# Two more load places for the first expert's chunks, and its first split set ahead of the last exponentials, in a one-core encoder block with 16 experts

## The chip, the cores and the metric

The kernel runs on one core of one Trainium2 chip. The metric is the device time of an execution in microseconds (us), the median of several runs. Engines are named PE (TensorE; PEld is its weight load), DVE (VectorE), ACT (ScalarE), POOL (GpSimd) and SP (SyncE). SP issues most DMAs, POOL the indirect ones.

## The reference

Two sets of 512 tokens of 1024 features in float32 go through one encoder layer: two groups of attention heads, their output projection added to the input, then a mixture of 16 experts in which every expert chooses its tokens.

```
def expert_choice_moe(h, w_router, w_gate, w_up, w_down):
    xf = h.reshape(n, d)                       # n = 512, d = 1024
    aff = jax.nn.softmax(jnp.einsum('nd,de->ne', xf, w_router), axis=-1)
    gates, idx = lax.top_k(aff.T, cap)         # cap = 2 * n / 16 = 64
    xe = xf[idx]
    hid = jax.nn.silu(jnp.einsum('ecd,edf->ecf', xe, w_gate)) * jnp.einsum('ecd,edf->ecf', xe, w_up)
    ye = jnp.einsum('ecf,efd->ecd', hid, w_down) * gates[..., None]
    y = jnp.zeros_like(xf).at[idx.reshape(-1)].add(ye.reshape(-1, d))

def encoder_layer(x, p):
    ...                                        # attention
    x = x + jnp.einsum('bse,ed->bsd', o, p['w_o'])
    h2 = rms_norm(x, p['norm_ffn'])
    return x + expert_choice_moe(h2, p['w_router'], p['w_gate'], p['w_up'], p['w_down'])
```

`w_gate`, `w_up` and `w_down` are 16 x 1024 x 1024 each, 201 MB together.

## The kernel before

There are four stages on one core: the input projection, attention, routing (`route`) and the experts (`experts`). No scheduler orders the work: each engine's program is written out by hand, the stages follow each other in it, and engines meet by semaphores.

**Two-part products.** Every large product is made of three in a faster format (`fp32r`): a tile is split into a higher part `hi` (ACT, a copy that rounds) and a lower part `lo` (raw minus `hi`), and hi x hi, lo x hi and hi x lo are added in PSUM.

**Chunks.** The experts' weights come in chunks of 128 x 2048 (1 MB, two blocks of 128 rows): 8 of gate and up per expert (`GU_CHUNKS`), in turns, then 4 of down. `load_chunk` issues one; those of expert 0's gate and up go as four DMAs of 32 partitions each, because its rows are stored in another order. Before the change there are `RING` = 6 places `raw` for loads, and 6 each of `hi` and `lo`. `split` of ACT (L2204) makes `hi`, `split` of DVE (L2282) makes `lo`, POOL the very first one (L2065). PE uses a chunk for 12 products of 512 columns (`gate_up`, `down`) and then counts `chunk_used`, which frees its place of `hi` and `lo`. `at(e, j)` numbers all chunks: 0 to 7 are expert 0's gate and up, from 8 on come expert 1's eight and the four of down of expert 0, and so on. ACT and DVE work `AHEAD` = 5 chunks ahead of PE. SP's `load` waits until `lo_done` has counted the chunk that had the place, six before.

**Routing.** Eight tiles of 128 tokens go through in the order 0, 1, 4, 5, 2, 6, 3, 7. For each, PE makes the output projection, DVE adds the residual (`x1`), SP stores it to `out`, ACT and POOL make the normalised rows `h2` (ACT `scale_rows`, L1766; POOL times the gain, L1605), SP stores them, and PE, ACT and DVE make the logits and the softmax (`exponentials`, L1760). SP issues chunks 0 to 5 among the tiles (`sync_program`, `load_chunk` of chunk j - 2 with tile j). After the last tile DVE finds the 64 largest per expert, and PE turns the lists. POOL then gathers expert 0's rows into `xe` (L2070), PE transposes them (L2184, L2091), ACT and DVE split them (into `hthi`, `htlo`), and PE's first expert product starts. While the lists are made, PE runs 24 transposes without use (L2180).

**Experts.** In the turn of expert e, PE makes gate and up (L2114 to L2116), eight transposes of the hidden rows of expert e - 1 (L2091) and down of e - 1 (L2128 to L2130). The next expert's rows are gathered by four DMAs (L2050), turned by DVE (`xt`, L2298) and split into `xehi` (ACT, L2212) and `xelo` (DVE, L2293). DVE makes `xelo` behind the lower part of the next expert's third chunk. POOL adds the rows of results to `out` by an indirect DMA (L2060).

**Memory.** `raw` lies in `arena`, where projected rows lay before; `hi` and `lo` over the buffers of attention and routing. `hi2` covers `h2` buffers, so ACT's third split waits for the last `h2` store.

Of the kernel before, what the change touches and what calls it, by code (L numbers as in the profile page):

```python
# [20 lines left out]
P = 128  # L21
# [30 lines left out]
RING = 6  # L52
# [69 lines left out]
def build(nc, a, out):  # L122
# [11 lines left out]
    with ExitStack() as ctx:  # L134
# [9 lines left out]
        k["ones"] = sb("ones", [P, 1])  # L144
        k["tab"] = sb("tab", [P, TS, TAB])
# [3 lines left out]
        k["gkp"] = sb("gkp", [P, TS, 2, PE_D])  # L149
        k["gcol"] = sb("gcol", [P, G_ROWS])  # L150
# [141 lines left out]
        moe["raw"] = [mm(f"raw{i}", [P, CHUNK]) for i in range(RING)]  # L292
        assert mm.at <= temps_at
# [1173 lines left out]
def route(phase, a, x_dram, k, wo, moe, ps, banks, o_dram, r_dram, out_rows, h2_rows, raw_loaded, attend_signals):  # L1467
# [40 lines left out]
    lmax_done, nbias_done, lexp_done, lrec_done, aff_done = sem("lmax_done"), sem("nbias_done"), sem("lexp_done"), sem("lrec_done"), sem("aff_done")  # L1508
    at_ready, at_done, merged, psteps, vsteps = sem("at_ready"), sem("at_done"), sem("merged"), sem("pool_steps_r"), sem("vector_steps_r")
# [32 lines left out]
    def sync_program(sp):  # L1542
# [13 lines left out]
        for u in range(T - 3, T):  # L1556
            store_rows(sp, u)
            store_scaled(sp, u)

    def gpsimd_pieces(pool):  # L1560
# [20 lines left out]
        def rest():  # L1581
# [7 lines left out]
            for j in range(1, T + 1):  # L1589
# [127 lines left out]
    def scalar_pieces(act):  # L1717
# [51 lines left out]
        def rest():  # L1769
# [16 lines left out]
            square_half(1)  # L1786
            exponentials(LAST)
# [178 lines left out]
    route_signals = {"merged": merged, "x1_stored": x1_stored, "h2_stored": h2_stored, "h2_done": h2_done}  # L1966
# [3 lines left out]
def experts(phase, a, k, moe, ps, banks, out, h2_dram, raw_loaded, route_signals):  # L1970
# [12 lines left out]
    merged, x1_stored, h2_stored, h2_done, rows_set = (  # L1983
        route_signals[n] for n in ("merged", "x1_stored", "h2_stored", "h2_done", "rows_set"))
# [13 lines left out]

    def loads_of(e, j):
        parts = P // SQUARE  # L2000
        if isinstance(e, int) and e == 0:
            return parts * (j // RING + 1)
        first = 2 if slot_of(e, j) < GU_CHUNKS - RING else 1
        return CHUNKS // RING * e + (j - DOWN_CHUNKS) // RING + 1 + (parts - 1) * first

    sem = phase.sem
    hi_done, lo_done, chunk_used = sem("hi_done"), sem("lo_done"), sem("chunk_used")
# [10 lines left out]
    def sync_program(sp):  # L2018
        need_split = sp.alloc_register("need_split")

        def load(e, j, name, of, i):
# [4 lines left out]
            load_chunk(sp, a, moe, raw_loaded, slot_of(e, j), name, of, i)  # L2026
# [12 lines left out]
    def gpsimd_program(pool):  # L2039
# [24 lines left out]
        pool.wait_ge(hi_done, 1)  # L2064
        pool.tensor_tensor(lo[0][:], raw[0][:], hi[0][:].bitcast(F32), ALU.subtract).then_inc(lo_done, 1)  # L2065
# [132 lines left out]
    def scalar_program(act):  # L2198
        def split(e, j):
            s = slot_of(e, j)  # L2200
            act.wait_ge(raw_loaded[s], 16 * loads_of(e, j))
            if not (isinstance(e, int) and e == 0 and j < RING):
                act.wait_ge(chunk_used, at(e, j) - RING + 1)
            act.activation(hi[s][:], raw[s][:], ACT.Copy).then_inc(hi_done, 1)  # L2204
# [38 lines left out]
        for j in range(RING):  # L2243
# [195 lines left out]
```

## Time and profile before

| | us |
|---|---|
| median of 3 runs | 1070.81 (1070.47 to 1073.97) |
| profiled execution | 1069.35 |
| its span, first to last instruction | 1067.5 |
| PE busy | 1022.0 (96%) |
| DVE busy | 888.9 (83%) |
| ACT busy | 771.1 (72%) |
| POOL busy | 494.8 (46%) |

The trace gives for every instruction its start in us from the span's start, its duration, and for idle time before it the operation that released it. Tile names stand without their numbers: `lo<-raw,hi` is any chunk's lower part, `h<-h,gffn` the rows `h2` times their gain. A DMA's time runs from the issue on SP or POOL to its landing. PEclk is the granted TensorE clock as a share of 2.4 GHz, the DMA share the mean busy share of the 16 DMA engines. Matmuls are shown longer than their distance, since they overlap. The attention stage ends near 350 us, routing runs to about 500, the experts to the end.

### The profile page before, as it was taken

How to read it: one execution, taken by the hardware profiler on the slowest of the kernel's cores; microseconds unless marked ns; L12 is line 12 of the kernel's file. 1: busy time of each engine (PE TensorE's matmuls, PEld its weight loads, DVE VectorE, ACT ScalarE, POOL GpSimd, SP SyncE). 2: the span in 40 equal slices, each digit the busy share in tenths (PEclk: the TensorE clock that was granted, in tenths of full speed). 3: DMA queues.
4: the chain of work that ended last, by engine and by line, in shares of the span. 5: the costliest groups of instructions: out<-in, count | busy, mean ns of one | idle time of the engine just before them, and what ended most of it. 6: DMA issues, size and time to landing. Idle time of an engine off the chain costs nothing.

```text
span 1067.5 us, 16503 instructions
## 1 busy us (share of the span) xinstructions
PE 1022.0 (96%) x5401; PEld 866.5 (81%) x5401; DVE 888.9 (83%) x1123; ACT 771.1 (72%) x1071; POOL 494.8 (46%) x458
## 2 busy tenths in 40 slices
PE   8999998999999999995999999999999999999995
PEld 7999987888788888884778888888787777877784
DVE  6787669999999954478999999889998999889992
ACT  7655568999999834335777887777877787778771
POOL 2476479555699754344442343224432343224021
PEclk9999999999999999996999999999999999999998
DMA  8132050211331379724999999999999999999992
GB/s 310 68 127 106 1 200 11 51 33 39 110 112 59 113 190 281 222 95 124 365 405 390 388 407 390 393 389 389 407 392 390 388 408 390 392 389 399 400 365 40
DMA packets 90128, 270.30 MB, mean 253 GB/s; under 512 B 16273, under 2 KB 24684, under 8 KB 89820
## 3 DMA queue, kind: packets, MB, share of 16 engines
q1 hardware_dynamic: 84272, 252.34, 62.9%
q0 software_dynamic: 5744, 17.29, 6.6%
q8 instruction: 28, 0.46, 0.2%
q14 instruction: 24, 0.20, 0.1%
q10 hardware_dynamic: 60, 0.01, 0.0%
HBM read 243.27 MB, written 26.35 MB: 253 GB/s over the span
## 4 chain that ended last, share of the span: by engine, by line
DVE 16%; DMA 15%; PE 12%; issue 8%; ACT 3%; POOLq 0%; DVEq 0%; POOL 0%; SPq 0%
DMA raw<-in_w_down 14%; DVE lo L2282 12%; PE ps L2114 3%; PE ps L2116 3%; PE ps L2115 3%; ACT hi L2204 2%; DVE h L2304 1%; DVE xelo L2293 1%; PE ps L2130 1%; PE ps L2128 1%; PE ps L2129 1%; DVE xt L2298 1%; DMA out<-y,give 1%; DMA xe<-h,idxT 0%; PE ps L2091 0%
## 5 line engine op out<-in xcount | busy, mean ns | idle before, releaser
L2282 DVE TENSOR_TENSOR lo<-raw,hi 128x2048 fp32r<-128x2048 f32 x191 | 431.9, 2287 | 40.5 <-ACT hi L2204 40.4
L2204 ACT ACTIVATE hi<-raw 128x2048 fp32r<-128x2048 f32 x192 | 367.6, 1919 | 109.3 <-DMA raw<-in_w_down 59.2
L2114 PE MATMUL ps<-hi,xehi 128*128 128x512 f32 x480 | 189.3, 394 | 7.6 <-DVE xelo L2293 6.6
L2116 PE MATMUL ps<-hi,xelo 128*128 128x512 f32 x480 | 187.1, 390 | 0.0
L2115 PE MATMUL ps<-lo,xehi 128*128 128x512 f32 x480 | 186.9, 389 | 0.0
L2045 POOL COPY take<-idx 128x4 uint32 (+1 forms) x15 | 29.0, 1935 | 208.1 <-DVE xt L2298 203.4
L2050 POOL DMA_INDIRECT xe<-h,take x60 | 104.9, 1748 | 25.1 <-issue 13.7
L2114 PEld LDWEIGHTS ps<-hi,xehi 128*128 128x128 f32 x480 | 90.1, 188 | 30.1 <-DVE lo L2282 9.1
L2116 PEld LDWEIGHTS ps<-hi,xelo 128*128 128x128 f32 x480 | 90.1, 188 | 18.9
L2115 PEld LDWEIGHTS ps<-lo,xehi 128*128 128x128 f32 x480 | 90.2, 188 | 18.0
L1417 DVE TENSOR_TENSOR probTlo<-ps,probThi 128x512 fp32r<-128x512 f32 x128 | 87.6, 684 | 14.1 <-ACT probThi L1372 11.5
L1363 ACT ACTIVATE prob<-ps,nmax 128x512 f32<-128x512 f32 x128 | 88.8, 693 | 7.8 <-DVE nmax L1421 6.7
L2128 PE MATMUL ps<-hi,hthi 128*128 128x512 f32 x240 | 93.5, 389 | 0.0
L2130 PE MATMUL ps<-hi,htlo 128*128 128x512 f32 x240 | 93.4, 389 | 0.0
L2129 PE MATMUL ps<-lo,hthi 128*128 128x512 f32 x240 | 93.4, 389 | 0.0
L1421 DVE TENSOR_REDUCE nmax<-ps 128x1 f32<-128x512 f32 x128 | 87.3, 683 | 4.2 <-PE ps L1255 2.5
L1268 PEld LDWEIGHTS ps<-ident,prob 128*128 128x128 f32 x512 | 62.6, 141 | 25.6 <-issue 7.9
L2060 POOL DMA_INDIRECT out<-y,give x15 | 32.2, 2145 | 110.1 <-ACT y L2240 110.1
L1372 ACT ACTIVATE probThi<-ps 128x512 fp32r<-128x512 f32 x128 | 76.8, 600 | 8.5 <-PE ps L1268 7.6
L1268 PE MATMUL ps<-ident,prob 128*128 128x128 f32 x512 | 77.1, 273 | 4.8 <-DVE probTlo L1417 4.4
L503 POOL TENSOR_TENSOR small<-small,minus_half 128x1 f32<-128x1 f32 (+4 forms) x40 | 66.1, 1653 | 3.3
L1286 PE MATMUL ps<-probThi,v 128*128 128x256 f32 x256 | 56.3, 301 | 0.0
(302 smaller groups left out, 2167.5 us busy)
## 6 DMA issues: line engine op xcount, KB each, us to landing
raw<-in_w_down SPq DMA_DIRECT2D x64, 1024.0 KB, 13.2
raw<-in_w_gate SPq DMA_DIRECT2D x60, 1024.0 KB, 11.2
raw<-in_w_up SPq DMA_DIRECT2D x60, 1024.0 KB, 11.5
w_raw<-in_w_in SPq DMA_DIRECT2D x8, 592.0 KB, 8.9
x<-in_x SPq DMA_DIRECT2D x8, 512.0 KB, 3.9
r<-reciprocal_sums SPq DMA_DIRECT2D x32, 128.0 KB, 2.9
attention_out<-pj SPq DMA_DIRECT2D x16, 256.0 KB, 2.5
woraw<-in_w_o SPq DMA_DIRECT2D x4, 1024.0 KB, 5.6
```

The lines of the kernel that those rows point to most:

```text
L1268: turned = pe.transpose(ps[:, T_BANKS[u % 2], cols], att["p"][u % 3][:, cols], k["ident"][:])
L1363: act.activation(att["p"][v % 3][:], ps[:, S_BANKS[v % 3], :], ACT.Exp, bias=att["nmax"][:, v:v + 1], accum_out=att["sum"][:, v:v + 1]).th ...
L1417: dve.tensor_tensor(ptlo[v // 2 % 2][:, :, cols], ps[:, T_BANKS[v % 2], :].rearrange("p (a c) -> p a c", a=TS), pthi[v // 2 % 2][:, :, col ...
L2050: pool.indirect_dma_start(xe[:, q * PART:(q + 1) * PART], None, h2_quarters, bass.IndirectOffsetOnAxis(moe["take"][:, q:q + 1], 0)).then_i ...
L2114: pe.matmul(ps[:, dst[n], :], rowhi[:, c, :], hi[w][:, cols], start=c == 0, stop=False)
L2115: pe.matmul(ps[:, dst[n], :], rowhi[:, c, :], lo[w][:, cols], start=False, stop=False)
L2116: last = pe.matmul(ps[:, dst[n], :], rowlo[:, c, :], hi[w][:, cols], start=False, stop=c == KD - 1)
L2128: pe.matmul(ps[:, Y[n], :], hthi[:, f, :], hi[w][:, cols], start=f == 0, stop=False)
L2129: pe.matmul(ps[:, Y[n], :], hthi[:, f, :], lo[w][:, cols], start=False, stop=False)
L2130: last = pe.matmul(ps[:, Y[n], :], htlo[:, f, :], hi[w][:, cols], start=False, stop=f == KD - 1)
L2204: act.activation(hi[s][:], raw[s][:], ACT.Copy).then_inc(hi_done, 1)
L2282: dve.tensor_tensor(lo[s][:], raw[s][:], hi[s][:].bitcast(F32), ALU.subtract).then_inc(lo_done, 1)
```

## The change

- Two more places for loads: `raw6` over the rotary tables and gains, which only the projection reads, and `raw7` over the start of the lower part of the output weights. `h` and `y` of the experts move over `raw7`, which is read for the last time before they are written.
- Chunks 6 and 7 go into these places and are issued in routing: chunk 6 ahead of the store of tile number 5, chunk 7 ahead of the store of tile number 6, when `wo_done` has counted the first group of products of the last tile. Each place has one load of expert 0 only; later chunks use six places again (`raw_of`).
- Expert 1's chunks 8 to 13 now follow into places 0 to 5, each when the lower part of chunk 0 to 5 is made. From chunk 14 on the rule is as before: the lower part of the chunk six earlier. The twelve loads of expert 1's turn are written out, the loop starts with expert 2.
- ACT makes `hi` of chunk 0 ahead of the last tile's exponentials and rows. POOL makes `lo` of chunk 0 ahead of the last tile's rows times gain, and `lo` of chunk 1, which DVE made before, behind them.

The diff, cut to its core:

```
@@ sync_program of route
         for u in range(T - 3, T):
+            c = RING + u - (T - 3)
+            if c < GU_CHUNKS:
+                if c > RING:
+                    sp.wait_ge(wo_done, 2 * LAST + 1)
+                load_chunk(sp, a, moe, raw_loaded, c, GATE_UP[c % 2], 0, c // 2)
             store_rows(sp, u)
             store_scaled(sp, u)
@@ gpsimd_pieces, rest
+                if u == LAST:
+                    pool.wait_ge(hi_done, 1)
+                    pool.tensor_tensor(moe["lo"][0][:], moe["raw"][0][:], moe["hi"][0][:].bitcast(F32), ALU.subtract).then_inc(lo_done, 1)
                 pool.wait_ge(h2_scaled, u + 1)
@@ scalar_pieces, rest
             square_half(1)
+            act.wait_ge(raw_loaded[0], 16 * (P // SQUARE))
+            act.activation(moe["hi"][0][:], moe["raw"][0][:], ACT.Copy).then_inc(hi_done, 1)
             exponentials(LAST)
@@ experts
+    def raw_of(e, j):
+        return j if isinstance(e, int) and e == 0 else j % RING
@@ sync_program of experts
-        for j in range(RING, GU_CHUNKS):
-            load(0, j, GATE_UP[j % 2], 0, j // 2)
-        with sp.Fori(1, EXPERTS) as e:
+        for j in range(CHUNKS):
+            sp.wait_ge(lo_done, j + 1 if j < RING else at(1, j) - RING + 1)
+            name, of, i = (GATE_UP[j % 2], 1, j // 2) if j < GU_CHUNKS else ("w_down", 0, j - GU_CHUNKS)
+            load_chunk(sp, a, moe, raw_loaded, raw_of(1, j), name, of, i)
+        with sp.Fori(2, EXPERTS) as e:
@@ gpsimd_program
-        pool.wait_ge(hi_done, 1)
-        pool.tensor_tensor(lo[0][:], raw[0][:], hi[0][:].bitcast(F32), ALU.subtract).then_inc(lo_done, 1)
+        pool.wait_ge(hi_done, 2)
+        pool.tensor_tensor(lo[1][:], raw[1][:], hi[1][:].bitcast(F32), ALU.subtract).then_inc(lo_done, 1)
@@ scalar_program
-        for j in range(RING):
+        for j in range(1, RING):
@@ vector_program
-        dve.wait_ge(lo_done, 1)
-        for j in range(1, RING):
+        dve.wait_ge(lo_done, 2)
+        for j in range(2, RING):
```

ACT at the end of routing, before; `x1_1` is the last tile, `aff1` its softmax, `hi0` the higher part of chunk 0:

```order
L1747 ACTIVATE sqo_123,smallo_115<-x1_1_127 128x512 [waits x1_done_p]
L1760 ACTIVATE aff1_118,smallo_115<-ps,smallo_115 128x16 [waits at_ready_p,aff_cleared_p,nbias_done_p]
L1766 ACTIVATE h2_1_134<-x1_1_127,smallo_115 128x8x4x32 [waits h2_stored1_p,r2_done_p]
L2204 ACTIVATE hi0_145<-raw0_139 128x2048 [waits raw_loaded0]
L2204 ACTIVATE hi1_146<-raw1_140 128x2048 [waits raw_loaded1]
L2204 ACTIVATE hi2_147<-raw2_141 128x2048 [waits raw_loaded2,h2_stored1_p,h2_stored0_p]
```

And now, with the line numbers of the changed kernel:

```order
L1762 ACTIVATE sqo_123,smallo_115<-x1_1_127 128x512 [waits x1_done_p]
L1803 ACTIVATE hi0_147<-raw0_139 128x2048 [waits raw_loaded0]
L1775 ACTIVATE aff1_118,smallo_115<-ps,smallo_115 128x16 [waits at_ready_p,aff_cleared_p,nbias_done_p]
L1781 ACTIVATE h2_1_134<-x1_1_127,smallo_115 128x8x4x32 [waits h2_stored1_p,r2_done_p]
L2225 ACTIVATE hi1_148<-raw1_140 128x2048 [waits raw_loaded1]
L2225 ACTIVATE hi2_149<-raw2_141 128x2048 [waits raw_loaded2,h2_stored1_p,h2_stored0_p]
```

The split of chunk 0 has moved ahead of the exponentials and the rows.

POOL at the same place, before (`pow` for the last norm, rows times gain, lower part 0, gather of expert 0's rows):

```order
L1566 TENSOR_TENSOR smallo_115<-smallo_115,minus_half 128x1 [waits pool_steps_r_p]
L1605 TENSOR_TENSOR h2_1_134<-h2_1_134,gffn_135 128x1024 [waits aff_done_p,h2_scaled_p]
L2065 TENSOR_TENSOR lo0_151<-raw0_139,hi0_145 128x2048 [waits hi_done_p]
L2070 DMA xe_157<-h2,idxT_166 128x1024 [waits h2_stored1_p,x1_stored1_p,idx_ready_p,h2_stored0_p,x1_stored0_p]
```

And now:

```order
L1578 TENSOR_TENSOR smallo_115<-smallo_115,minus_half 128x1 [waits pool_steps_r_p]
L1616 TENSOR_TENSOR lo0_153<-raw0_139,hi0_147 128x2048 [waits hi_done_p]
L1620 TENSOR_TENSOR h2_1_134<-h2_1_134,gffn_135 128x1024 [waits aff_done_p,h2_scaled_p]
L2086 TENSOR_TENSOR lo1_154<-raw1_140,hi1_148 128x2048 [waits hi_done_p]
L2091 DMA xe_159<-h2,idxT_162 128x1024 [waits h2_stored1_p,x1_stored1_p,idx_ready_p,h2_stored0_p,x1_stored0_p]
```

Lower part 0 stands ahead of the rows, and a lower part 1 between the rows and the gather.

SP from the load of chunk 5 on, before:

```order
L1527 DMA h2<-h2_0_133 128x1024 [waits h2_done_p]
L1523 DMA out<-x1_1_127 128x1024 [waits x1_done_p]
L1527 DMA h2<-h2_1_134 128x1024 [waits h2_done_p]
L1523 DMA out<-x1_0_126 128x1024 [waits x1_done_p]
L1527 DMA h2<-h2_0_133 128x1024 [waits h2_done_p]
L1523 DMA out<-x1_1_127 128x1024 [waits x1_done_p]
L1527 DMA h2<-h2_1_134 128x1024 [waits h2_done_p]
L1461 DMA raw0_139<-in_w_gate 32x2x1024 [waits lo_done_p,raw_loaded0]
L1461 DMA raw0_139<-in_w_gate 32x2x1024 x3
L1461 DMA raw1_140<-in_w_up 32x2x1024 [waits lo_done_p,raw_loaded0]
L1461 DMA raw1_140<-in_w_up 32x2x1024 x3
```

And now:

```order
L1534 DMA h2<-h2_0_133 128x1024 [waits h2_done_p]
L1467 DMA raw6_145<-in_w_gate 32x2x1024 x4
L1530 DMA out<-x1_1_127 128x1024 [waits x1_done_p]
L1534 DMA h2<-h2_1_134 128x1024 [waits h2_done_p]
L1467 DMA raw7_146<-in_w_up 32x2x1024 [waits wo_done_p]
L1467 DMA raw7_146<-in_w_up 32x2x1024 x3
L1530 DMA out<-x1_0_126 128x1024 [waits x1_done_p]
L1534 DMA h2<-h2_0_133 128x1024 [waits h2_done_p]
L1530 DMA out<-x1_1_127 128x1024 [waits x1_done_p]
L1534 DMA h2<-h2_1_134 128x1024 [waits h2_done_p]
L1470 DMA raw0_139<-in_w_gate 128x2x1024 [waits lo_done_p]
L1470 DMA raw1_140<-in_w_up 128x2x1024 [waits lo_done_p]
```

Chunks 6 and 7 have moved ahead of the stores of `x1`, and expert 1's chunks follow the last `h2` store, without chunks of expert 0 between.

## Rows read from the trace of the kernel before

**Rows 1.** Busy PE, PEld, DVE, ACT, POOL (count); clock, DMA share, GB/s
```profile
458.00:470.00 12.00, 12.00 (x66) 10.03 (x65) 7.03 (x20) 5.72 (x10) 5.51 (x6) 1.00 0.23 89
502.00:506.00 4.00, 4.00 (x21) 4.00 (x20) 3.94 (x9) 1.79 (x1) 1.12 (x1) 0.50 0.89 228
541.00:734.00 193.00, 192.86 (x871) 159.78 (x870) 178.77 (x108) 151.93 (x113) 72.67 (x41) 1.00 1.03 395
734.00:1010.00 276.00, 270.69 (x1216) 222.25 (x1216) 252.79 (x152) 214.33 (x160) 88.18 (x51) 1.00 1.03 394
```

**Rows 2.** Waits of TensorE's products, 720 to 1020: us, times, longest
```profile
PE ps L2114 <- DVE xelo L2293: 6.1, 9, 0.8
```

**Rows 3.** Waits of ScalarE, 540 to 610, then 650 to 1010
```profile
ACT hi L2204 <- PE ps L2116: 7.2, 11, 0.9
...
ACT hi L2204 <- DMA raw<-in_w_down: 48.4, 42, 2.5
```

**Rows 4.** Timeline of TensorE: start, us; the eight transposes of three experts
```profile
638.53 1.04 PE L2091 MATMUL ps<-ident,h 128*128 128x128 f32 x8
...
672.07 1.04 PE L2091 MATMUL ps<-ident,h 128*128 128x128 f32 x8
...
1016.23 1.04 PE L2091 MATMUL ps<-ident,h 128*128 128x128 f32 x8
```

**Rows 5.** Timeline of SyncE's queue: stores of the last tiles, chunks 6 to 8
```profile
458.31 0.43 SPq L1523 DMA_DIRECT2D out<-x  x1
...
493.81 0.32 SPq L1527 DMA_DIRECT2D h<-h  x1
498.36 1.93 SPq L1461 DMA_DIRECT2D raw<-in_w_gate  x4
505.26 1.90 SPq L1461 DMA_DIRECT2D raw<-in_w_up  x4
507.64 0.42 SPq L1464 DMA_DIRECT2D raw<-in_w_gate  x1
```

**Rows 6.** Timeline of ScalarE at the end of routing; in brackets idle time
```profile
489.86 0.36 ACT L1760 ACTIVATE aff<-ps,smallo 128x16 f32<-128x16 f32 x1 [2.25 <-DVE smallo L1855]
...
496.48 7.31 ACT L2204 ACTIVATE hi<-raw 128x2048 fp32r<-128x2048 f32 x4 [1.53 <-issue]
507.39 0.38 ACT L2252 ACTIVATE hthi<-ps 128x256 fp32r<-128x256 f32 x1 [3.59 <-PE ps L2184]
```

**Rows 7.** Timeline of GpSimd at the end of routing
```profile
491.43 2.35 POOL L1605 TENSOR_TENSOR h<-h,gffn 128x1024 f32<-128x1024 f32 x1 [2.62 <-ACT h L1766]
493.75 4.52 POOL L2065 TENSOR_TENSOR lo<-raw,hi 128x2048 fp32r<-128x2048 f32 x1
502.28 1.12 POOL L2070 DMA_INDIRECT xe<-h,idxT  x1 [4.01 <-DVE idxT L2329]
```

**Rows 8.** Timeline of VectorE: expert 0's token numbers; its run of lower parts
```profile
501.03 0.37 DVE L2329 TENSOR_SCALAR idxT<-ps 64x16 uint32<-64x16 f32 x2
...
509.28 17.70 DVE L2282 TENSOR_TENSOR lo<-raw,hi 128x2048 fp32r<-128x2048 f32 x8
```

**Rows 9.** Issue to landing of `raw` loads: 540 to 570, 507 to 512
```profile
DMA to landing us min/median/max: 8.8/9.4/11.3
...
DMA to landing us min/median/max: 6.9/8.0/8.7
```

**Rows 10.** Issue to landing: `woraw`'s four loads; gathers into `xe`, 500 to 530
```profile
DMA to landing us min/median/max: 5.1/5.6/7.1
...
DMA to landing us min/median/max: 4.6/7.2/8.0
```

**Rows 11.** Timeline of TensorE: warm-up, turning of expert 0's rows, first product
```profile
501.34 5.38 PE L2180 MATMUL ps<-ident 128*128 128x128 f32 x24
506.91 0.66 PE L2184 MATMUL ps<-ident,xe 128*128 128x128 f32 x4 [0.19 <-DMA xe<-h,idxT]
...
508.49 0.47 PE L2114 MATMUL ps<-hi,hthi 128*128 128x512 f32 x1 [0.48 <-DVE htlo L2351]
```

More of the change, by code:

```diff
@@ L144, in build @@
         k["ones"] = sb("ones", [P, 1])
+        tables_at = (nc.sbuf_base + 63) // 64 * 64
         k["tab"] = sb("tab", [P, TS, TAB])
@@ L149, in build @@
         k["gkp"] = sb("gkp", [P, TS, 2, PE_D])
+        assert nc.sbuf_base >= tables_at + CHUNK * 4
         k["gcol"] = sb("gcol", [P, G_ROWS])
@@ L292, in build @@
         moe["raw"] = [mm(f"raw{i}", [P, CHUNK]) for i in range(RING)]
+        moe["raw"] += [Map(tables_at)("raw6", [P, CHUNK]), Map(w_in_end)("raw7", [P, CHUNK])]
         assert mm.at <= temps_at
@@ L311, in build @@
         moe["give2"] = mm("give2", [P, 2], U32)
+        assert mm.at <= w_in_end
+        mm.at = w_in_end
+        moe["h"] = mm("h", [P, FF])
+        moe["y"] = mm("y", [P, D])
+        assert mm.at == w_in_end + CHUNK * 4
+        moe["xelo"] = mm("xelo", [P, KD, P], F32R)
+        moe["silu"] = mm("silu", [P, FF])
+        moe["hthi"] = mm("hthi", [P, KD, P], F32R)
+        moe["htlo"] = mm("htlo", [P, KD, P], F32R)
+        moe["xt"] = mm("xt", [P, D])
         assert mm.at <= end, (mm.at, end)
-        raw_loaded = [ctx.enter_context(nc.semaphore(f"raw_loaded{i}")) for i in range(RING)]
+        raw_loaded = [ctx.enter_context(nc.semaphore(f"raw_loaded{i}")) for i in range(GU_CHUNKS)]
         wo_loaded = ctx.enter_context(nc.semaphore("wo_loaded"))
@@ L1982, in experts @@
     TAIL = GU_CHUNKS + CHUNKS * LAST
-    merged, x1_stored, h2_stored, h2_done, rows_set = (
-        route_signals[n] for n in ("merged", "x1_stored", "h2_stored", "h2_done", "rows_set"))
+    hi_done, lo_done, merged, x1_stored, h2_stored, h2_done, rows_set = (
+        route_signals[n] for n in ("hi_done", "lo_done", "merged", "x1_stored", "h2_stored", "h2_done", "rows_set"))
     out_halves = out.rearrange("t (h c) -> (t h) c", h=2)
@@ L2001, in loads_of @@
         if isinstance(e, int) and e == 0:
-            return parts * (j // RING + 1)
-        first = 2 if slot_of(e, j) < GU_CHUNKS - RING else 1
-        return CHUNKS // RING * e + (j - DOWN_CHUNKS) // RING + 1 + (parts - 1) * first
+            return parts
+        return CHUNKS // RING * (e - 1) + j // RING + 1 + parts
     sem = phase.sem
-    hi_done, lo_done, chunk_used = sem("hi_done"), sem("lo_done"), sem("chunk_used")
+    chunk_used = sem("chunk_used")
     route_ready, gates_ready, idx_ready = sem("route_ready"), sem("gates_ready"), sem("idx_ready")
@@ L2199, in split @@
         def split(e, j):
-            s = slot_of(e, j)
-            act.wait_ge(raw_loaded[s], 16 * loads_of(e, j))
+            s, r = slot_of(e, j), raw_of(e, j)
+            act.wait_ge(raw_loaded[r], 16 * loads_of(e, j))
             if not (isinstance(e, int) and e == 0 and j < RING):
                 act.wait_ge(chunk_used, at(e, j) - RING + 1)
-            act.activation(hi[s][:], raw[s][:], ACT.Copy).then_inc(hi_done, 1)
+            act.activation(hi[s][:], raw[r][:], ACT.Copy).then_inc(hi_done, 1)
         def high(dst, b, ready, n, done):
```

16 lines of the change are left out of this document (5 added, 11 removed).

## The prediction

> **What bounds the kernel now.** I read the stretches first [rows 1]. From 541 to 1010 us, nearly half of the span, the DMA engines are full (share 1.03, 394 to 395 GB/s). TensorE is also at 192.86 of 193 us until 734, but at 270.69 of 276 us after that. So two limits lie close together: TensorE sets the pace first, the weight transfers later.
>
> The waits say the same. From 720 us on, TensorE's first product of an expert waits nine times for VectorE's `xelo` [rows 2]. VectorE writes `xelo` after the lower part of the next expert's third chunk, and that one waits for ScalarE's higher part. Up to 610 us ScalarE's splits wait for TensorE to free `hi`; from 650 us on they wait for landings [rows 3]. An expert's eight transposes are a good marker of pace [rows 4]: 672.07 - 638.53 = 33.54 us where TensorE sets it. From 672.07 to 1016.23 are ten experts: 344.16 us, against 335.4 at that pace. **So 8.8 us is all that an earlier stream of weights can win back**, and only if TensorE starts no later. After 1016 the end is TensorE's own work and does not move against it.
>
> **The change part by part.** I number expert 0's gate and up chunks 0 to 7 and go on with expert 1's from 8.
>
> 1. *Chunks 6 and 7 are issued in the routing stage.* Now they go out at 498.36, when GpSimd has made the first lower part, and at 505.26, after VectorE's first [rows 5]. Four parts each take 1.9 us to issue. In the changed kernel chunk 6 goes ahead of the store at 458.31, where the DMA engines are busy 0.23 of the time [rows 1], and chunk 7 after the last tile's first group of products. The stores behind them on SyncE's queue are needed only by the gather at 502.28, twenty us later; that cover costs nothing. What leaves is two chunks of the crowded stretch after 498.
>
> 2. *Higher part 0 ahead of the last exponentials.* ScalarE is idle for 2.25 us from 487.6 to 489.86, and one split takes 1.9 us (7.31 us for four, less overlap) [rows 6]. It ends about 489.5 and the exponentials start as before: 0.
>
> 3. *Lower part 0 on GpSimd ahead of the last `h2` rows.* GpSimd then works 489.6 to 494.1 (4.52 us), makes the rows until 496.45 (2.35 us, now 491.43 to 493.78), then lower part 1 until 501.0 [rows 7]. Two things hang on it. The store of `h2`, issued at 493.81 now [rows 5], goes at 496.5, 2.7 us later. ScalarE's third split, which starts 2.7 us after that issue (496.48), moves to 499.2, and four splits end at 506.5; the next work waits until 507.39 [rows 6], so 0.9 us of cover is left: 0. If the store lands over 0.9 us later than that, every us more delays TensorE. The gather of expert 0's rows is queued behind lower part 1. It waits for its indices, which VectorE has written at 501.4 [rows 8], and starts at 502.28: 0.4 us of cover, cost 0; any lengthening beyond this goes into TensorE's start one to one.
>
> 4. *VectorE loses lower part 1.* It is no gain: VectorE still makes part 2 at 502.9, then waits for the gathered rows, and its run of eight lower parts starts at 509.28 as now [rows 8]. The two waits of TensorE near 531 and 535 us hang on that run; they stay.
>
> 5. *Expert 1's loads go out earlier.* Chunk 8 waits for lower part 0 alone, but stands behind the `h2` store: 496.8. Chunk 9 goes when lower part 1 is done, 501.1, chunk 10 at 505.2, against 507.64 for chunk 8 now [rows 5]. Chunks 11 to 13 need VectorE's run, 17.70 us for eight, and go at 511.6, 513.8 and 516.0. Chunk 14 needs lower part 8 in both kernels: same time. By then the queue should be empty, which it isn't now.
>
> **How far ahead can the stream get?** This is the step that I chose on. It would be two chunks plus their slow four-part form, over 5 us. But chunks from 14 on are issued when a place is free, that is at TensorE's pace, in both kernels, and nothing lands sooner than a lone chunk takes. Of the chunks issued from 540 to 570 the quickest lands after 8.8 us [rows 9]. Lone loads of the same 1024 KB, of `woraw`, take 5.1 to 5.6 us [rows 10]; I take 5.6, its upper value, since gathers run beside the weights too. So the lead is 8.8 - 5.6 = **3.2 us**, bounds 8.8 - 5.1 = 3.7 and, where a gather comes first as well, 8.8 - 6.2 = 2.6. From there the queue is never empty again, so the lead lasts until it is spent on the nine waits, of 8.8 us together: it removes the first three to four.
>
> The Trainium skill (DMA: Bandwidth & Descriptors, "Anatomy of one DMA — SWDGE (gpsimd) path") gives a DMA a fixed part of about 2.0 us and bytes over 436 GB/s, an estimate of 4.4 us for such a chunk. The rows show 5.1 at best; by the rule the lead would be 4.4 us, and the time 1067.3.
>
> **What chunk 9 costs the gather.** The gather of expert 0's rows takes 4.6 us (502.28 to 506.9) on nearly empty queues, and TensorE starts 0.19 us after it [rows 10, 11]. In the changed kernel chunk 9 was issued 1.2 us before it. At 395 GB/s a chunk keeps the queues for 2.7 us, from some 502.5 to 505.2, and the gather's 512 KB, 1.3 us at that rate, would flow from about 504 on. That is 0 to 1.2 us of delay for TensorE's first product (508.49). I take **0.9 us**, nearer to the upper end, because the later gathers, of 128 KB each on full queues, take 7.2 us in the median although they are a quarter of the size.
>
> The skill's same page ("Queues, rings and completion order") says that an engine drains a whole packet of some 9 to 17 descriptors from one queue before it turns to the next. By that rule chunk 9's share passes whole and the delay is the full 1.2 us; that no row here shows.
>
> **Sum.** -3.2 + 0.9 = -2.3 us, with 0 for splits, stores and VectorE. The profiled execution took 1069.35 us (span 1067.5), so it would be about 1067.0. The median of the runs is 1070.81, 1.5 us above the profiled one; the same difference gives **1068.5 us**. Bounds: -3.7 + 0 and -2.6 + 1.2, that is 1067.1 to 1069.4.
>
> **The rivals.** *A larger lead.* The `h2` store of 512 KB has landed 2.7 us after its issue (493.81 to ScalarE's 496.48); another 512 KB at the full rate make 4.0 us. If a lone chunk lands in 4.5, between this and 5.1, the lead is 4.3, and without a delay of the gather the time is 1066.5. Against it: none of the four loads of `woraw` came under 5.1. The skill's fixed part, above, points to this case; by it and with no delay the time would be 1066.4.
>
> *No lead.* The chunks issued in 507 to 512 took 6.9 to 8.7 us with one or two ahead of them [rows 9]. If about 8 us is what a chunk takes in this stage whatever is queued, the lead is 8.8 - 8 = 0.8 and the gather takes it back: 1070.9. The same time comes if VectorE, and not the landings, holds `xelo` back: then an earlier stream changes nothing. Against that: ScalarE's waits for landings in [rows 3].
>
> *Slower, by a late gather and a slow clock.* A quarter gather would take 4.6 - 1.0 = 3.6 us alone and takes 7.2 on a full queue. If the first gather is held up as much by chunk 9, TensorE starts 3.6 us later, which alone eats the 3.2. TensorE would also stand idle that long after its warm-up transposes, which run from 501.34 for 5.38 us [rows 11], at a granted clock of 0.50 [rows 1] (1.2 GHz). If the clock falls again in that gap, the first products pay as the transposes did: about 5.4 us at half speed are 2.7 us lost. Time 1070.8 + 0.4 + 2.7 = 1073.9. It decides from the gap at which the clock falls; the gaps of 0.19 and 0.48 us there now let it stand, and 0.9 more should.
>
> **How the numbers follow.** The sum above 0.55, own range 1067.1 to 1069.4; the larger lead 0.20 at 1066.5; no lead 0.14 at 1070.9; the slower one 0.11 at 1073.9. Predicted is 1068.5. The range of 8 in 10 takes in the first three but for their tails: 1066.0 to 1071.5. A measurement of this kernel can tell about 0.3%, 3.2 us: faster is under 1067.6, slower over 1074.0. Faster gets one in six of the first case (0.09) and nearly all of the second (0.19): 0.28. Slower gets half of the last, rounded up: 0.06. Within it 0.66.
>
> **What would show it.** Right: chunks 6 and 7 issued from 458 on and before 486; exponentials still at 489.9; gather issued at 502.3, landing 507 to 508; TensorE's first product at 508.5 to 509.7; the quickest chunk from 540 to 570 landing after 5.2 to 6 us; experts at 33.54 us until well past 800; five to six waits for `xelo` in place of nine, and 8.8 us of loss down to about 5.6. The forecast is wrong if TensorE's first product is over 2 us late (part 3, or the gather), if the minimum landing stays above 8 us, or if TensorE waits for something new, such as the two reused places, after 541.

## The result

| | before | after |
|---|---|---|
| median, us | 1070.95 (20 runs) | 1073.89 (20 runs) |
| profiled span, us | 1067.5 | 1072.1 |
| first expert product of TensorE | 508.49 | 513.77 |
| TensorE's waits for `xelo`, 720 to 1020 us | 9 | 8 |

The changed kernel is slower: ratio 1.0026, 95% interval 1.0015 to 1.0036, or 2.9 us. Forecast was 1068.5 with a range of 1066.0 to 1071.5, so the time lies outside it and on the other side of before. The ratios here and below leave out three slow executions, of 1287 us (fourth experiment), 2648 us (fifth) and 3643 us (sixth).

Where does it go? VectorE's timeline at the end of routing, after (start in us, duration, then the instruction; `smallo` holds the routing's small columns). L1869 takes the largest logit, L1872 multiplies it by the root, which gives the bias of the exponentials:

```profile
490.60 0.17 DVE L1869 TENSOR_REDUCE smallo<-ps 128x1 f32<-128x16 f32 x1 [1.16 <-PE ps L1695]
490.81 4.33 DVE L1872 TENSOR_TENSOR smallo<-smallo 128x1 f32<-128x1 f32 x1
```

The same product before the change:

```profile
489.67 0.16 DVE L1855 TENSOR_TENSOR smallo<-smallo 128x1 f32<-128x1 f32 x1
```

L1872 works on 128 x 1 elements and takes **4.33 us**, where it took 0.16. In the changed kernel it also takes 0.16 us for the tile before. GpSimd's timeline at the same time:

```profile
490.63 4.49 POOL L1616 TENSOR_TENSOR lo<-raw,hi 128x2048 fp32r<-128x2048 f32 x1 [0.69 <-ACT hi L1803]
496.75 2.35 POOL L1620 TENSOR_TENSOR h<-h,gffn 128x1024 f32<-128x1024 f32 x1 [1.62 <-ACT h L1781]
499.06 4.50 POOL L2086 TENSOR_TENSOR lo<-raw,hi 128x2048 fp32r<-128x2048 f32 x1
507.59 1.12 POOL L2091 DMA_INDIRECT xe<-h,idxT  x1 [4.03 <-DVE idxT L2350]
```

GpSimd's lower part 0 (L1616) starts at 490.63 and ends at 495.12. VectorE's product starts 0.18 us later and ends 0.02 us after it. ScalarE then shows who waits:

```profile
488.66 1.89 ACT L1803 ACTIVATE hi<-raw 128x2048 fp32r<-128x2048 f32 x1
495.18 0.36 ACT L1775 ACTIVATE aff<-ps,smallo 128x16 f32<-128x16 f32 x1 [4.62 <-DVE smallo L1872]
...
502.14 7.31 ACT L2225 ACTIVATE hi<-raw 128x2048 fp32r<-128x2048 f32 x4 [3.67 <-issue]
```

The exponentials start at 495.18 after 4.62 us of idle time, where [rows 6] had 489.86. Everything behind them is 5.3 to 5.7 us later than before: the `h2` rows at 496.75 (491.43 in [rows 7]), the gather at 507.59 (502.28), the last four splits at 502.14 (496.48). TensorE's timeline (warm-up transposes, turning of expert 0's rows, first products):

```profile
506.65 4.21 PE L2201 MATMUL ps<-ident 128*128 128x128 f32 x24
512.20 0.66 PE L2205 MATMUL ps<-ident,xe 128*128 128x128 f32 x4 [1.34 <-DMA xe<-h,idxT]
...
513.77 0.47 PE L2135 MATMUL ps<-hi,hthi 128*128 128x512 f32 x1 [0.48 <-DVE htlo L2372]
514.08 0.40 PE L2136 MATMUL ps<-lo,hthi 128*128 128x512 f32 x1
514.31 0.40 PE L2137 MATMUL ps<-hi,htlo 128*128 128x512 f32 x1
```

The first product comes at 513.77, 5.28 us later than in [rows 11]. Of these, 1.14 are there before the change has done anything, as SyncE's queue shows (store of `h2` rows, chunk 6, last `h2` store, chunks 8 and 9):

```profile
459.04 0.34 SPq L1534 DMA_DIRECT2D h<-h  x1
459.43 2.23 SPq L1467 DMA_DIRECT2D raw<-in_w_gate  x4
...
499.12 0.32 SPq L1534 DMA_DIRECT2D h<-h  x1
499.49 0.43 SPq L1470 DMA_DIRECT2D raw<-in_w_gate  x1
503.59 0.38 SPq L1470 DMA_DIRECT2D raw<-in_w_up  x1
```

The `h2` store at 459.04 comes ahead of every moved instruction; before it was at 457.92. I take this as a difference between executions: below, a kernel without the new places has it at 459.29 and one with them at 457.95. The rest, 5.28 - 1.14 = 4.14 us, agrees with the 4.17 us by which L1872 is longer.

And the weights? Issue to landing of `raw` loads issued from 540 to 570 us, and TensorE's waits for `xelo` (us in total, times, longest):

```profile
DMA to landing us min/median/max: 5.0/6.7/9.3
...
PE ps L2135 <- DVE xelo L2314: 5.7, 8, 0.8
```

The quickest landing is 5.0 us, where [rows 9] had 8.8, so the stream did get ahead; yet eight waits are left of nine. To count what a lead is worth I use the distances between an expert's eight transposes, as in [rows 4]: an expert whose rows are there in time takes 33.54 us, a late one 34.6. What fourteen such distances in a row take over 33.54 each is TensorE's loss:

| kernel | first expert product | experts at 33.54 us | loss, us |
|---|---|---|---|
| before | 508.49 | 5 | 8.8 |
| after | 513.77 | 6 | 8.1 |
| lower part behind (first experiment) | 508.37 | 6 | 8.0 |
| moves only, no new places (second) | 515.64 | 7 | 6.9 |
| one input (third) | 512.59 | 7 | 7.2 |
| four pieces (fourth) | 510.57 | 6 | 7.5 |
| nothing held beside lower part 0 (fifth) | 511.13 | 6 | 7.6 |
| the same, lower part 1 on VectorE (fifth) | 508.34 | 6 | 7.4 |
| one place | 509.67 | 6 | 7.3 |
| short loads early, 16 partitions | 509.48 | 6 | 8.0 |
| short loads late, 16 partitions | 508.39 | 8 | 6.0 |
| short loads late, all partitions | 509.13 | 10 | 3.7 |

Each row is one execution. After against before, the places win 0.7 us of the 3.2 forecast, and the moved lower part loses 4.1. Over all kernels with two places and full loads the loss is 7.2 to 8.1, so the places win 0.7 to 1.5 us; where TensorE starts within 0.2 us of before, it is 0.7 (first experiment) and 1.4. A late start takes something off by itself: the second experiment has no places and loses 6.9, with 1.2 us more in the stretch from its first product to the first transposes, which the table does not count.

### The profile page after: what moved, and what is told of

Its sections match the earlier page's. It is cut to its first block, busy times and chain, and to the rows that moved or that the text cites. A ratio compares the mean times of both kernels' runs of the same rounds, so it can differ in the third digit from the quotient of the medians.

```text
span 1072.1 us, 16425 instructions
## 1 busy us (share of the span) xinstructions
PE 1020.9 (95%) x5401; PEld 865.6 (81%) x5401; DVE 890.9 (83%) x1122; ACT 771.3 (72%) x1071; POOL 499.6 (47%) x459
## 4 chain that ended last, share of the span: by engine, by line
DVE 16%; DMA 15%; PE 11%; issue 7%; ACT 2%; POOLq 0%; DVEq 0%; POOL 0%; SPq 0%
DMA raw<-in_w_down 14%; DVE lo L2303 12%; PE ps L2135 3%; PE ps L2137 3%; PE ps L2136 3%; ACT hi L2225 2%; DVE h L2325 1%; PE ps L2151 1%; PE ps L2149 1%; PE ps L2150 1%; DVE xelo L2314 1%; DMA raw<-in_w_gate 1%; DVE xt L2319 1%; DMA out<-y,give 1%; DMA xe<-h,idxT 0%
## 6 DMA issues: line engine op xcount, KB each, us to landing
raw<-in_w_up SPq DMA_DIRECT2D x60, 1024.0 KB, 11.5
```

## Experiments

**1. The lower parts back, the places kept.** Theory A: GpSimd's instruction keeps VectorE's product from running. Theory B: the transfers in routing cost the time.

```
-                if u == LAST:
-                    pool.wait_ge(hi_done, 1)
-                    pool.tensor_tensor(moe["lo"][0][:], ...).then_inc(lo_done, 1)
@@ gpsimd_program: lower part 0 here again; vector_program: `for j in range(1, RING)`
```

> The changed kernel, with lower part 0 on GpSimd behind the last rows times gain again and lower part 1 on VectorE, as before; the two places and the early higher part stay. Theory A (GpSimd's lower part 0 holds VectorE's bias product, 4.33 us for 0.16): that product takes 0.16 to 0.2 us again, the exponentials follow the higher part within 2 us, TensorE's first expert product comes at 508.5 to 509.7 in place of 513.8, and the time is 1070.95 (before) less the lead of the weights that is left, 0.6 to 3.2 us: 1067.8 to 1070.4. Theory B (the loads issued in routing and chunk 9 cost the time, through transfers): the first product stays over 2 us late, time 1073 to 1074.

VectorE's bias product and TensorE's first expert product in that run:

```profile
489.70 0.16 DVE L1869 TENSOR_TENSOR smallo<-smallo 128x1 f32<-128x1 f32 x1
```

```profile
508.37 0.47 PE L2132 MATMUL ps<-hi,hthi 128*128 128x512 f32 x1 [0.48 <-DVE htlo L2369]
```

The product takes 0.16 us and TensorE starts at 508.37. The time is **1068.54 us** against 1070.34 for before, ratio 0.9984 (0.9970 to 0.9998): of the kernels here that compute the reference's results, the only one whose interval lies below before. Higher part 0 still stands early on ScalarE in it, so that move costs nothing. Theory B falls.

**2. Only the moves, no new places.** The kernel before, with `hi` of chunk 0 and the two lower parts as in the change, and chunks 6 and 7 loaded late.

```
+                if u == LAST:
+                    pool.wait_ge(hi_done, 1)
+                    pool.tensor_tensor(moe["lo"][0][:], ...).then_inc(lo_done, 1)
                 pool.wait_ge(h2_scaled, u + 1)
@@ and hi_done, lower part 1 and the loops over RING as in the change
```

> The kernel before with only the moves: higher part 0 ahead of the last exponentials, lower part 0 on GpSimd ahead of the last rows, lower part 1 on GpSimd behind them; no new places, chunks 6 and 7 loaded late as before. Theory A: the bias product takes 4.2 to 4.5 us, first expert product 4.1 us later than before (512.6), time 1070.95 + 4.1 = 1075.0, within 1. Theory B: bias product may be long, but the time is within 1 us of before, 1070 to 1072.

Its VectorE product, GpSimd's lower part 0 and gather, TensorE's turning of the gathered rows and first product, and SyncE's store of the tile before and chunks 6 and 7:

```profile
491.03 4.34 DVE L1861 TENSOR_TENSOR smallo<-smallo 128x1 f32<-128x1 f32 x1
```

```profile
490.86 4.49 POOL L1605 TENSOR_TENSOR lo<-raw,hi 128x2048 fp32r<-128x2048 f32 x1 [0.69 <-ACT hi L1792]
...
507.81 1.12 POOL L2076 DMA_INDIRECT xe<-h,idxT  x1 [4.02 <-DVE idxT L2335]
```

```profile
514.07 0.66 PE L2190 MATMUL ps<-ident,xe 128*128 128x128 f32 x4 [2.16 <-DMA xe<-h,idxT]
...
515.64 0.77 PE L2120 MATMUL ps<-hi,hthi 128*128 128x512 f32 x1 [0.31 <-DVE htlo L2357]
```

```profile
459.29 0.34 SPq L1528 DMA_DIRECT2D h<-h  x1
...
499.86 2.23 SPq L1461 DMA_DIRECT2D raw<-in_w_gate  x4
503.86 1.74 SPq L1461 DMA_DIRECT2D raw<-in_w_up  x4
```

4.34 us again, and 1075.52 us, ratio 1.0044 (1.0032 to 1.0057). The loss is in the moves. The first product at 515.64 is later than the 512.6 expected: 1.4 us are the difference between executions (459.29 against 457.92), and the gather takes 514.07 - 507.81 = 6.26 us to TensorE's use, against 4.6 before. Chunk 7, in four parts, was issued 4 us ahead of it. It landed only at 513.14. That this chunk is the reason was not tested by itself.

**3. One tensor input in place of two.** VectorE's bias product and its product with 1/sum as `tensor_scalar`, the second factor a scalar per partition.

```
-            dve.tensor_tensor(nbias(j), lmax(j), r2(j), ALU.mult)
+            dve.tensor_scalar(nbias(j), lmax(j), r2(j), None, ALU.mult)
-            dve.tensor_tensor(pair[:, cols], pair[:, cols], lrec(j).to_broadcast([P, EXPERTS]), ALU.mult)
+            dve.tensor_scalar(pair[:, cols], pair[:, cols], lrec(j), None, ALU.mult)
```

> The changed kernel, with VectorE's bias product and its product of the exponentials with 1/sum written as a product of a tile with a scalar per partition (one tensor input) in place of two tensor inputs; the same numbers come out. Theory A with the port taken only against two inputs in SBUF: both take under 0.3 us beside lower part 0, the first expert product comes at 509 to 510.3, the lead of 0.6 to 3.2 us is kept: 1067.8 to 1070.6. Theory A2 (any such VectorE arithmetic on SBUF is held while GpSimd works): the bias product still takes over 4 us, time 1073.9. Theory C (the delay is not in the port but in the signal or the value of the root that GpSimd makes just before): no change either, 1073.9.

VectorE (bias product, 1/sum, product with it) and GpSimd (lower part 0, rows):

```profile
490.45 0.21 DVE L1872 TENSOR_SCALAR smallo<-smallo 128x1 f32<-128x1 f32 x1
491.19 0.16 DVE L1877 RECIPROCAL smallo<-smallo 128x1 f32<-128x1 f32 x1 [0.52 <-ACT aff L1775]
491.39 3.44 DVE L1879 TENSOR_SCALAR aff<-aff,smallo 128x16 f32<-128x16 f32 x1
```

```profile
490.28 4.52 POOL L1616 TENSOR_TENSOR lo<-raw,hi 128x2048 fp32r<-128x2048 f32 x1 [0.69 <-ACT hi L1803]
494.98 2.34 POOL L1620 TENSOR_TENSOR h<-h,gffn 128x1024 f32<-128x1024 f32 x1 [0.18 <-DVE aff L1879]
```

Half right. The 128 x 1 product takes 0.21 us in the middle of lower part 0, and so does the reciprocal in 0.16: neither the root's value nor its signal was late, and theory C falls. But the next one, 128 x 16 with a single tensor input, takes 3.44 us and ends at 494.83, with lower part 0 (494.80). So one input is not enough to be free. The time is 1072.26, ratio 1.0019 (1.0006 to 1.0032), above the 1067.8 to 1070.6 expected: the hold has moved one instruction down.

The Trainium skill has this rule (SBUF — State Buffer, "SBUF: two separate sides"): VectorE and GpSimd share one pair of ports, and whichever of the two starts first keeps it for its whole instruction, against a VectorE operation with two SBUF inputs or in a two-port performance mode. "Who interferes with whom" names `tensor_scalar` among the operations that can enter such a mode. The trace agrees with the length of the hold: ends within 0.03 us of GpSimd's, for two inputs and for the 128 x 16 `tensor_scalar`, and no hold for the 128 x 1 one. That the 128 x 16 one is held because it enters such a mode no run here shows. By that rule TensorE's first product would have come out some 4 us late, and the prediction did not weigh it.

**4. Lower part 0 in four pieces.** The times and the profile are from two runs of one kernel.

```
-                    pool.tensor_tensor(moe["lo"][0][:], moe["raw"][0][:], ...).then_inc(lo_done, 1)
+                    for q in range(4):
+                        part = slice(q * BANK, (q + 1) * BANK)
+                        low = pool.tensor_tensor(moe["lo"][0][:, part], moe["raw"][0][:, part], ...)
+                    low.then_inc(lo_done, 1)
```

> The changed kernel, with GpSimd's lower part 0 in four instructions of 512 columns each, some 1.1 to 1.2 us a piece; nothing else. Theory A (VectorE's product waits for the end of the GpSimd instruction that is running): the bias product takes 0.2 to 1.3 us, the product with 1/sum as much, the first expert product comes at 510 to 511.7, time 1070 to 1072. Theory A3 (it waits until GpSimd has nothing to do): 4.3 us and 1073.9 as it is. Theory C: 1073.9.

> One look at the kernel whose lower part 0 is made in four instructions of 512 columns. Theory A: VectorE's bias product takes at most 1.3 us (to the end of the piece that runs), the product of the exponentials with 1/sum as well, and the first expert product comes 22.5 to 25 us after the last x1, in place of 26.5.

VectorE (bias product, product with 1/sum), and GpSimd's four pieces in one row:

```profile
490.08 1.10 DVE L1875 TENSOR_TENSOR smallo<-smallo 128x1 f32<-128x1 f32 x1
...
491.90 0.52 DVE L1882 TENSOR_TENSOR aff<-aff,smallo 128x16 f32<-128x16 f32 x1
```

```profile
489.91 4.94 POOL L1618 TENSOR_TENSOR lo<-raw,hi 128x512 fp32r<-128x512 f32 x4 [0.69 <-ACT hi L1806]
```

A piece takes some 1.24 us, and the two products take 1.10 and 0.52 us: each waits for the end of the piece that runs, and gets its turn between two pieces. The hold is bounded by the GpSimd instruction that runs. Time 1070.44, ratio 0.9998 (0.9985 to 1.0011): 3.4 us better than the changed kernel, with TensorE's first product 24.0 us after the last `x1` (510.57 - 486.55), in place of 26.5.

**5. No held instruction beside lower part 0.** The bias product with one input, and the last tile's division on ScalarE.

```
+            act.wait_ge(lrec_done, LAST + 1)
+            act.activation(pair[:, cols], pair[:, cols], ACT.Copy, scale=lrec(LAST)).then_inc(aff_done, 1)
             scale_rows(LAST)
```

> The changed kernel, but for the last tile VectorE's bias product has one tensor input (128x1 times a scalar per partition) and the exponentials are divided by their sum on ScalarE (a copy with a scale) in place of VectorE; the same numbers come out. So no VectorE instruction of a kind seen to be held stands beside GpSimd's lower part 0. Theory A: no VectorE instruction takes over 0.3 us there, rows follow lower part 0 at once, the gather is issued 15.5 to 16.5 us after the last x1 (as before: 16.2), TensorE's first product 22 to 22.8 us after it, and chunks 8 and 9 go out at 497 and 501: time 1067.5 to 1069.0. If the port is not the cause, the first product stays 4 us late and the time is 1072 to 1074.

VectorE (bias product, 1/sum, first two-input step of the merge of the lists) and GpSimd (lower part 0, rows, lower part 1):

```profile
491.28 0.21 DVE L1876 TENSOR_SCALAR smallo<-smallo 128x1 f32<-128x1 f32 x1
492.02 0.17 DVE L1883 RECIPROCAL smallo<-smallo 128x1 f32<-128x1 f32 x1 [0.52 <-ACT aff L1775]
...
501.38 1.11 DVE L1928 SCALAR_TENSOR_TENSOR places<-idx,places 48x64 f32<-48x64 uint32 x1
```

```profile
491.11 4.52 POOL L1616 TENSOR_TENSOR lo<-raw,hi 128x2048 fp32r<-128x2048 f32 x1 [0.69 <-ACT hi L1803]
495.59 2.34 POOL L1620 TENSOR_TENSOR h<-h,gffn 128x1024 f32<-128x1024 f32 x1
497.90 4.51 POOL L2094 TENSOR_TENSOR lo<-raw,hi 128x2048 fp32r<-128x2048 f32 x1
```

Beside lower part 0 nothing is held, and the rows follow it at 495.59, as the prediction had drawn it. But the merge step at 501.38 takes 1.11 us and ends at 502.49, when lower part 1 (to 502.41) does. The first product comes 23.4 us after the last `x1`; the time is 1070.08, ratio 1.0004 (0.9994 to 1.0014). Both are above what was expected (22 to 22.8 us, 1067.5 to 1069.0), and the gather goes out 17.2 us after the last `x1`, not 15.5 to 16.5. Then the same kernel with lower part 1 on VectorE:

> The kernel with the last normalisation on ScalarE, but lower part 1 is made by VectorE as before the change; lower part 0 stays early on GpSimd. In the run before, VectorE's first two-input step of the merge (48x64) took 1.11 us in place of 0.22 and ended with GpSimd's lower part 1. Theory A: it takes 0.22 again, TensorE's first product comes 22.3 to 22.7 us after the last x1 in place of 23.4, time 1068.3 to 1069.5 against 1070.1. If lower part 1 did not hold it, the step stays near 1.1 us and the time stays at 1070.

```profile
499.57 0.22 DVE L1928 SCALAR_TENSOR_TENSOR places<-idx,places 48x64 f32<-48x64 uint32 x1
```

The step takes 0.22 us and TensorE's first product comes 22.4 us after the last `x1`, as before the change. Time 1069.63, ratio 0.9999 (0.9986 to 1.0012), 0.1 us above the expected range. The trace confirms the second hold; the times of these two kernels overlap. Without a hold the kernel is level with before in the median, and its profiled span is 1066.1 us against 1067.5.

**6. How much lead can there be?** First with one place less, from the kernel of the first experiment.

```
 def raw_of(e, j):
-    return j if isinstance(e, int) and e == 0 else j % RING
+    if isinstance(e, int) and e == 0:
+        return j if j <= RING else 0
+    return (j + 1) % RING
```

> The kernel of the first experiment (lower part 0 behind the rows) with only one more place: chunk 6 is loaded in routing, chunk 7 goes into place 0 when lower part 0 is made, expert 1's chunks follow one place later. Theory L1 (what is loaded ahead stays ahead): half the lead, so half the gain of 1.8 us over before: 1069.4. Theory L2 (the places cap it: from chunk 14 on a load is issued when a place is free, in this stretch the transfers run dry, and what the second place won is lost by 560 us): chunk 14 lands after 7 to 8 us in place of 5.1, but chunk 24 after 5.8 to 6.5, chunk 30 after 10.4 to 10.7, and the time is that of two places within 0.5: 1068.0 to 1069.0.

1069.29 us, ratio 0.9995 (0.9985 to 1.0004). By time L1 (1069.4) fits better, but it overlaps with two places; the loss in the table is 7.3 us, within the 7.2 to 8.1 of two places. So no lead that lasts shows for the second place. L2's landings missed: chunk 14 after 8.59 us (expected 7 to 8), chunk 24 after 6.66 (5.8 to 6.5), chunk 30 after 9.80 (10.4 to 10.7), and the time is 0.3 us above its range.

Then with fewer bytes where the queue is short. Here is what the DMA engines moved in three stretches (busy time and count of PE, PEld, DVE, ACT, POOL; clock, DMA share, GB/s), before:

```profile
524.00:540.00 16.00, 14.46 (x67) 11.42 (x66) 16.00 (x13) 11.66 (x12) 8.12 (x5) 1.00 1.03 405
540.00:556.00 16.00, 16.00 (x72) 13.26 (x71) 14.34 (x8) 11.73 (x8) 4.87 (x3) 1.00 1.02 407
556.00:572.00 16.00, 16.00 (x75) 13.27 (x74) 14.73 (x11) 13.64 (x11) 7.83 (x5) 1.00 1.03 404
```

and in the first experiment:

```profile
524.00:540.00 16.00, 14.45 (x67) 11.43 (x66) 16.00 (x13) 11.65 (x12) 8.12 (x5) 1.00 0.98 381
540.00:556.00 16.00, 16.00 (x72) 13.24 (x72) 14.33 (x8) 11.73 (x8) 4.98 (x3) 1.00 0.95 357
556.00:572.00 16.00, 16.00 (x76) 13.30 (x75) 14.75 (x11) 13.56 (x12) 7.71 (x5) 1.00 1.02 394
```

Before moves 404 to 407 GB/s in a row and catches up with TensorE: issue to landing falls from 11.5 us (chunk 16) to 8.8 (chunk 24). The kernel with the places moves 381, 357 and 394. It has no backlog to draw on, since from chunk 14 on the loads are issued at TensorE's pace in both (chunk 24 at 552.29 and 552.18). In 48 us that is 16 x (24 + 50 + 10) = 1.34 MB less, or 3.3 us at 405 GB/s: the kernel before catches up by so much.

```
-    sp.dma_start(dst, src).then_inc(raw_loaded[slot], 16)
+    sp.dma_start(dst[0:rows], src[0:rows]).then_inc(raw_loaded[slot], 16)
@@ rows = 16 for j in (6, 7) of expert 1's turn, else 128
```

> The kernel of the first experiment, but expert 1's last two chunks of gate and up (14 and 15) load only 16 of 128 partitions, so 1.75 MB less: results of expert 1 are not those of the reference, every other instruction is the same. That is 1.84 MB / 395 GB/s = 4.6 us less transfer, just where the queue is short. Theory L1: the lead grows by 4.6 us and takes away most of the losses of TensorE after 750 us (8.6 us by distances of products): 1068.5 - 4.6 = 1063.9. Theory L2: nearly all of it is lost as idle DMA engines by 560 us: chunk 30 lands at most 1 us sooner than with full loads, time 1067.3 to 1068.5.

```profile
524.00:540.00 16.00, 14.48 (x67) 11.42 (x66) 16.00 (x11) 11.67 (x10) 8.12 (x5) 1.00 0.72 246
540.00:556.00 16.00, 16.00 (x72) 13.26 (x71) 14.33 (x10) 12.03 (x8) 4.18 (x2) 1.00 0.95 356
```

The rate falls to 246 GB/s in the first stretch and is the same again in the next. The two short loads land 2.8 and 2.6 us after their issue, and chunk 16 after 4.9 in place of 7.1; at chunk 21 nothing of it is left (5.07 us, 5.12 in the first experiment). Chunk 30 lands after 10.4 us (10.5). Time 1069.21, ratio 0.9990 (0.9982 to 0.9999), against 1068.54, where TensorE started 1.1 us earlier: **1.84 MB less to load, and nothing gained.** L1 falls for this stretch; the time is 0.7 us above the range that L2 gave. The medians of before itself, in four such series, went from 1069.73 to 1070.95.

The same with `rows = 16` in expert 5's turn:

> The same two short loads, but of expert 5 (chunks 62 and 63, near 680 us), where a chunk takes 12 us to land and several wait in the queue; the results of expert 5 are not those of the reference. Theory L1 and L2 alike: the queue stays full, the lead of 4.6 us is kept: landings of the chunks after 64 take 7 to 8 us in place of 12, TensorE's first five or six waits for xelo (773 to 911 us) are gone, time 1068.5 - 4.6 = 1063.9, within 0.8. Together with the run before it this tells whether the same bytes are worth something early. If both give 1068, TensorE is held by something else than landings.

1066.44 us, ratio 0.9968 (0.9956 to 0.9981): 2.1 us gained on the first experiment where 4.6 were expected. The short loads themselves were slow: from 654 to 670 us 348 GB/s flowed in place of 404. So once more with short loads over all partitions:

```
+    if rows < P:
+        dst, src = dst[:, 0:1, 0:BANK], src[:, 0:1, 0:BANK]
```

> As the run with two short loads of expert 5, but each short load takes 512 columns of one block in all 128 partitions (256 KB) in place of 16 partitions, since those of 16 partitions went at 348 GB/s in 654 to 670 us where full ones went at 404. Results of expert 5 are not those of the reference. 1.57 MB less, 4.0 us at 395 GB/s. If the queue is full there and the lead lasts, chunk 70 lands 3 to 4 us sooner after its issue than the 11.7 us of the first experiment, and the time is 1068.5 - 3.5 = 1065.0, within 0.8. If it stays at 1066.4, something else than the form of the short loads took the half of their lead.

Issue to landing of the loads issued from 680 to 700 us in the first experiment:

```profile
DMA to landing us min/median/max: 11.2/11.7/13.5
```

and with the short loads, with TensorE's waits for `xelo`:

```profile
DMA to landing us min/median/max: 7.8/8.3/9.3
...
PE ps L2140 <- DVE xelo L2319: 2.6, 4, 0.8
```

The median landing falls from 11.7 to 8.3 us, four waits for `xelo` are left of eight, and the time is 1065.97 (ratio 0.9961, 0.9946 to 0.9975), 2.6 us under the first experiment and 1 us above what I expected, 0.2 outside the range; the loss by the table falls by 4.3, and the span by 3.5 (TensorE started 0.76 us later in this execution). So of these loads the bytes saved counted where the queue was deep, and not where it was short.

## Why the prediction was wrong

*The reading of the kernel* holds. TensorE's pace of 33.54 us, the later one set by landings, and the 8.8 us as all that a lead can win are what the table of losses shows.

*Part 1*, chunks 6 and 7: right, issued at 459.43 and 479.39. *Part 2*, the early higher part: right by itself; the first experiment keeps it, and its exponentials start when VectorE's bias is there.

*Part 3 is the step that failed.* It put lower part 0 on GpSimd beside VectorE and costed GpSimd's queue, ScalarE's splits, the store and the gather, but not what GpSimd's instruction does to VectorE's one, which it put at nothing. Part 2's "the exponentials start as before: 0", true for the higher part alone, became 4.17 us with part 3, on the path that sets the end. The prediction took durations as if they didn't depend on the neighbour. The trace of before had a sign: VectorE's lower part L1807 (128 x 512) takes 0.69 us in each of the six tiles where no GpSimd instruction runs beside it, but 0.91 to 1.22 in the five where a GpSimd `tensor_tensor` (L1571) does, such as:

```profile
453.72 1.22 DVE L1807 TENSOR_TENSOR otlo<-gained,othi 128x512 fp32r<-128x512 f32 x1
```

```profile
453.08 1.30 POOL L1571 TENSOR_TENSOR osq<-osq 128x512 f32<-128x512 f32 x1 [6.06 <-ACT osq L1731]
```

A wait of 0.66 us to the end of L1571 leaves 0.56, near the 0.69 that it takes alone. Part 3's own covers (0.9 us at the splits, 0.4 at the gather) never came into play: splits and gather moved with everything else.

*Part 4*, nothing from VectorE: right; the run of eight lower parts takes 17.71 us as before.

*Part 5, the lead*, was mis-sized: forecast 3.2, measured 0.7 in the changed kernel and in the first experiment, and 1.5 at most in any kernel with two places. By medians the first experiment is 1.8 us under before, interval 0.2 to 3.2, which can't tell these apart. The latency step was right (5.0 and 5.1 us against 8.8), and at chunk 24 the lead is there: it lands 5.84 us after its issue in the first experiment, before 8.75. The sentence that failed is "From there the queue is never empty again, so the lead lasts". From the landing of chunk 24 to that of chunk 30 before took 18.85 us, the first experiment 20.89. I took one moment's difference in latency for a store of bytes, while one kernel ran at full rate and the other at TensorE's pace. The latency of a lone load was also read too narrowly: the four `woraw` loads of [rows 10] took 5.1 to 7.1 us, and 5.6 is their median, not their upper value.

*The gather's 0.9 us* was nothing in the changed kernel: there chunk 9 went out 4.0 us ahead of it (503.59, 507.59) and TensorE took its rows 4.61 us after the issue, as before. With chunk 9 2.5 us ahead, in experiment 5, it was 4.59 us. A distance of 1.2 us, as I had assumed, occurred in no run. A longer gather there was once, the 6.26 us of the second experiment, with chunk 7 still in flight.

*The rivals.* The slower one, at 1073.9, met the time by luck and not by its way: the gather was not slowed by chunk 9 but issued late, and the clock did not fall in the gap behind the warm-up. TensorE stood idle for 1.34 us ahead of the turning, and the granted clock is 1.00 (2.4 GHz) from 510 to 516 us. Its price for a late start was right in kind, a late start costs nearly one to one: in the second experiment, too, 7.15 us of later start gave 6.5 us of longer span. "No lead" was closest on the stream's side: its 0.8 us is about what is left, though its reason, that a chunk takes about 8 us whatever is queued, is refuted by the 5.0 us. The larger lead needed a lone chunk in 4.5 us; the quickest full load of any kernel here from chunk 8 on took 4.8. The estimate of 4.4 us rests on a fit that the Trainium skill (DMA: Bandwidth & Descriptors, "Anatomy of one DMA — SWDGE (gpsimd) path") makes for DMAs issued by GpSimd; these loads are SyncE's, and none of them came under 4.8.

With both terms as measured the sum is 4.1 - 0.7 = +3.4 us, against 2.9 by the medians (interval 1.6 to 3.9).

## What to carry to other kernels

Before an instruction is moved to GpSimd, or in time beside VectorE, list VectorE's instructions that will run in that stretch; each with two SBUF inputs, however small, can wait until the GpSimd instruction that is running ends (and so did a 128 x 16 `tensor_scalar`), and where it feeds the path that sets the end, that is the price. If it must stand there, cut the GpSimd instruction into pieces or give VectorE's step another form or engine. A lead in a stream of loads is worth only what is still ahead when the queue is next deep: compare the rate moved from here to there, not the latency at one moment.

## What the runs showed of the hardware

- A VectorE product of 128 x 1 took 4.33 and 4.34 us beside a GpSimd `tensor_tensor` of 4.5 us and 0.16 alone. Beside pieces of 1.24 us it took 1.10.
- `tensor_scalar` from SBUF was held at 128 x 16 (3.44 us), not at 128 x 1 (0.21 us); a reciprocal of 128 x 1 (0.16 us) and the searches for the eight largest were not held.
- Loads to 16 of 128 partitions slowed the whole stream: 348 GB/s over 16 us, where loads to all partitions, short ones among them, gave 402 to 404.
